# Gated attention: the compressed turn and the lump of value products move ahead of the transposition on TensorE's queue

## What is computed

```python
s_c = einsum('bqghd,bngd->bghqn', qb, kc) * scale      # 31 compressed keys
p_c = masked_softmax(s_c, cmp_end <= t)
o_c = einsum('bghqn,bngd->bqghd', p_c, vc)
...
p_s = masked_softmax(einsum(qb, k_g) * scale, valid_s)  # selected keys
o_s = einsum('bghqk,bgqkd->bqghd', p_s, v_g)
...
p_w = masked_softmax(einsum(qb, kw) * scale, valid_w)   # window keys
o_w = einsum('bghqk,bkgd->bqghd', p_w, vw)
out = gb[..., 0:1] * o_c + gb[..., 1:2] * o_s + gb[..., 2:3] * o_w
```

## Time and profile before

| | us |
|---|---|
| median of 3 runs | 2261.6 (2260.36 to 2263.69) |
| profiled execution, its own time | 2260.86 |
| its span | 2259.6 |
| TensorE busy in the span | 2201.7 (97%) |
| VectorE, ScalarE, GpSimd busy | 1341.6, 560.7, 199.8 |
| the stage of the change, from the first logits to the last lump | 853.6 to 1020.7 |

### The profile page before, as it was taken

The page is one execution under the profiler, slowest core; times in us unless marked ns, Lnnn a source line. Parts: engine busy times, 40 slices in busy tenths (PEclk is TensorE's granted clock), DMA queues, the critical chain, the costliest instruction groups (busy, mean ns, idle before and its releaser), DMA issues.

```text
span 2259.6 us, 29545 instructions
## 1 busy us (share of the span) xinstructions
PE 2201.7 (97%) x10990; PEld 1583.5 (70%) x10990; DVE 1341.6 (59%) x3432; ACT 560.7 (25%) x1421; POOL 199.8 (9%) x210
## 2 busy tenths in 40 slices
PE   9999999999999998999999999999999999999988
PEld 7776578888888885558888888888867633343333
DVE  6777766656566667876665665767776522222224
ACT  2223431101001206772110000323573111111111
POOL 0013430000000002330000000000020011111101
PEclk9999999999999999999999999999999999999999
DMA  5211032232222320002222222232205999999997
GB/s 212 75 57 47 13 124 86 83 94 86 82 94 88 121 75 20 1 1 75 83 86 94 84 85 94 77 103 64 63 13 219 356 416 423 423 422 424 423 425 325
DMA packets 60207, 346.54 MB, mean 153 GB/s; under 512 B 9248, under 2 KB 10144, under 8 KB 42208
## 3 DMA queue, kind: packets, MB, share of 16 engines
q1 hardware_dynamic: 55360, 335.03, 39.7%
q0 software_dynamic: 3840, 6.46, 0.8%
q10 hardware_dynamic: 864, 3.15, 0.3%
HBM read 337.59 MB, written 17.30 MB: 157 GB/s over the span
## 4 chain that ended last, share of the span: by engine, by line
PE 89%; DMA 6%; DVE 3%; ACT 1%; issue 1%; DVEq 0%; SPq 0%; POOLq 0%; ACTq 0%
PE bank L636 30%; PE bank L642 8%; PE bank L649 8%; PE bank L657 8%; PE bank L3097 7%; DMA places<-in_experts 5%; PE bank L3105 4%; PE bank L625 2%; PE bank L3054 2%; PE bank L1125 2%; PE bank L1137 2%; PE bank L1109 2%; PE bank L3070 1%; PE bank L499 1%; PE bank L731 1%; PE bank L1332 1%
## 5 line engine op out<-in xcount | busy, mean ns | idle before, releaser
L3097 PE MATMUL bank<-places,xT 128*64 128x512 f32 x832 | 185.1, 593 | 12.9 <-DMA places<-in_experts 12.9
L3306 DVE TENSOR_SCALAR square<-bank,mt 128x256 f32<-128x256 f32 x32 | 15.5, 484 | 284.8 <-ACT rope L3209 284.8
L3097 PEld LDWEIGHTS bank<-places,xT 128*64 128x64 f32 x832 | 60.4, 137 | 132.2 <-issue 118.9
L1992 DVE TENSOR_TENSOR third<-first,bank 128x256 f32<-128x256 f32 x106 | 44.6, 421 | 151.3 <-PE bank L636 150.5
L636 PE MATMUL bank<-u,ring 128*128 128x256 f32 x540 | 130.3, 381 | 1.1 <-DVE y_ab L2026 1.1
L636 PE MATMUL bank<-h,ring 128*128 128x256 f32 x512 | 121.0, 379 | 0.0
L636 PE MATMUL bank<-h_sums,w_sum 128*128 128x256 f32 x512 | 120.9, 379 | 0.0
L636 PEld LDWEIGHTS bank<-u,ring 128*128 128x128 f32 x540 | 101.2, 190 | 17.8 <-issue 3.3
L2685 POOL TENSOR_SCALAR exps<-exps,small,gates 128x128 f32<-128x128 f32 (+1 forms) x64 | 55.9, 874 | 652.9 <-DVE small L2479 652.9
L636 PE MATMUL bank<-u_mlp,ring 128*128 128x256 f32 x480 | 113.4, 379 | 0.0
L636 PE MATMUL bank<-u_mlp_sums,w_sum 128*128 128x256 f32 x480 | 113.4, 379 | 0.0
(11 more groups left out here) (560 smaller groups left out, 4394.0 us busy)
## 6 DMA issues: line engine op xcount, KB each, us to landing
places<-in_experts SPq DMA_DIRECT2D x56, 2048.0 KB, 35.0
ring<-in_dense SPq DMA_DIRECT2D x216, 512.0 KB, 4.2
places<-in_experts SPq DMA_DIRECT2D x40, 1024.0 KB, 23.1
x<-in_experts SPq DMA_DIRECT2D x11, 1024.0 KB, 24.8
w<-in_experts SPq DMA_DIRECT2D x10, 1024.0 KB, 29.6
consts<-in_experts SPq DMA_DIRECT2D x10, 1024.0 KB, 30.4
x<-in_experts SPq DMA_DIRECT2D x4, 2048.0 KB, 37.3
consts<-in_consts SPq DMA_DIRECT2D x1, 2310.5 KB, 16.5
```

Source lines behind the costliest of these rows:

```text
L3097: ins = k.pe.matmul(bank[a * CAP:(a + 1) * CAP, :], xT[:, kk % 4, kk // 4, :], w[:, (2 * (kk % 2) + a) * EH:(2 * (kk % 2) + a + 1) * EH], ...
```

## The change

In each step of `pe_nsa` the compressed turn (at A3) and the lump (at A0 and A3) are issued behind the unit's logits and ahead of the transposition, where before they came behind the transposition. The lists of the other engines stay as they are.

```diff
@@ pe_nsa
         if m < 8 and at == 0:
             pe_cmp_logits(k, m)
+        if m < 8 and at == 3:
+            pe_cmp_turn(k, m)
+        if step >= 4 and (step - 4) % 3 == 2:
+            pe_nsa_values(k, NSA_UNITS[step - 4][-1])
         if 0 <= step - 3 < len(NSA_UNITS):
             pe_nsa_turn(k, step - 3)
-        if m < 8 and at == 3:
-            pe_cmp_turn(k, m)
         if m < 7 and at == 4:
             pe.wait_ge(s["scaled"], SCALED["c"] + CQ + m + 2)
             pe_rope(k, k.ch7, ("cq", m + 1), k.yc[:, CQ + m + 1, :])
         if m < 8 and at == 4:
             pe_cmp_values(k, m)
-        if step >= 4 and (step - 4) % 3 == 2:
-            pe_nsa_values(k, NSA_UNITS[step - 4][-1])
```

## The result

The changed kernel takes 2274.8 us in the median of 7 runs (2270.09 to 2279.51), the kernel before 2261.6 (7 runs, 2259.3 to 2267.78): a ratio of 1.0051, interval 1.0033 to 1.0068, slower by 13.2 us. The profiled execution took 2271.68. I had forecast 2268.9, and no more than 2272. The direction and the mechanism held, the size did not: 13.2 us instead of 7.3.

What follows compares the result with a forecast made beforehand. No engine is full, TensorE is nearest; loops +5.7, opening +0.6, and end +0.5 and +0.5 sum to +7.3 us on the profiled 2260.86, or 2268.9 us for the median; range 2263.5 to 2272.

Steps and rivals of the forecast that it cites:

- the loop: Each m: TensorE to ScalarE to TensorE twice, 20.98 us against 20.16 on average before; seven loops cost +5.7 us.
- the opening: First A3, no lump: the compressed turn moves ahead and waits for VectorE's weights, delaying the first rotary product by 0.6 us.
- the end: At m = 7: +0.5 us waiting for `u`, and +0.5 from the compressed values on, 13.1 us against 12.5.
- A3 comes back at the rotary product: The 1.56 us saved at A3 return as a 1.54 us stall for `p_cmpT` before A4's rotary product: net nothing.
- A0's delay reaches the A3 lump: A0's transposition starts 2.30 us later, ScalarE with it; the A3 lump starts at 901.78, not about 900.64.
- Rival 2: Both shifts cancel, about 2262.5 us, needing ScalarE's 6.07 us to be 1.1 shorter; chance 0.15 together with a shorter loop.
- ScalarE's idle time before the A0 copies: At A0 ScalarE stands idle about 2 us, so that masks up to 2 us late cost nothing.
- the wait for `u`: At m = 7 the compressed values also wait for `u`, copied 0.49 us behind `p_cmpT`: +0.5 us.
- Rival 3: Three stalls per m could lower the clock; a tenth of the stage at half speed costs some 15 us, 2284; chance 0.03.
- The bounds: Without delays the loop is 20.7 and the sum +5.3; with ScalarE 0.1 us longer per stretch, 21.2 and +8.7.
- Rival 1: The gap is simply filled: TensorE's 13.0 us of waits at A3 and A0 are gained, 2249.2 us; chance 0.08, wholly or partly.

Runs made afterwards that it cites:

- one: Against the changed kernel, the A0 lump goes back behind its transposition, so only A3 has the new order: 2262.4 us, ratio 0.9994 to the kernel before.
- two: Against the changed kernel, compressed turn and A3 lump go back behind the transposition, only the A0 lump stays ahead: 2263.0 us, ratio 0.9997.
- five: The changed kernel run again, unaltered, for a larger sample beside the kernel before: 2273.3 us, ratio 1.0053.
- six: The changed kernel plus seven keep-warm products (matmuls nobody reads) in front of the last compressed values alone: 2271.0 us, ratio 1.004.
- eight: Only A3's lump ahead, plus ScalarE's `p_cmpT` copy moved before its A3 copies and `u` right behind them, against the kernel before: 2251.8 us, ratio 0.9954.
- seven: The changed kernel, both lumps ahead, plus ScalarE's `p_cmpT` copy before its A3 copies and `u` right behind them: 2260.5 us, ratio 0.9992 to the kernel before.

## Why the prediction was wrong in size and right in cause

The path was right: a loop from TensorE to ScalarE and back, twice per m. Of the sum, +7.3 us, these terms were mis-sized: the loop (20.98 forecast, 21.21 measured: +1.6 us over seven), the opening (-0.25), the end at full clock (+0.1), and the clock behind the last gap, which the sum put at nothing (+1.4). That gives the stage's 10.2. The 3 us that are left up to 13.2 are most likely the clock's spread from one execution to the next, for which my range had little room.

*A3 comes back at the rotary product.* Right: 1.35 us of wait there at each of the seven, 1.54 forecast, and A3 alone changes nothing (one).

*A0's delay reaches the A3 lump.* Right: block 3's transposition waits 0.61 us, the lump 0.32, in sum 0.93 where I had 1.1. Rival 2 (both shifts cancel) holds only if one half is left out (one, two).

*The loop of 20.98 us.* The term that missed by most. It is 21.21: rotary product to A0 lump 5.89 instead of 5.72 (it takes 0.93 us instead of 0.86 after a wait, and the lump follows the compressed logits 1.03 behind instead of 0.94), from a transposition to the copies twice 0.64 instead of 0.59; ScalarE's stretches and the delays came out within 0.03. The two terms that were short were read from places where TensorE's work ran through without a wait. Seven times 0.23 is 1.6 us. ScalarE's idle time before the A0 copies, which I had put at about 2 us, is 2.68.

*The opening and the end.* The opening cost 0.35 instead of 0.6. At the end the wait for `u` is there, 0.5 us as forecast (1.84 against 1.35), and the rest is +0.6 at full clock, where I had 0.5.

*Rival 3, the clock.* I wrote that the new stalls are no longer than 1.4 us. That was wrong by my own sum: a stall of 1.54 plus 0.5 for `u` at m = 7 is 2.0, and the trace shows 1.84. Behind it the clock fell, +1.4 us (five, six). The size that I gave the rival, 15 us, was ten times too large; it took place once and not in every m.

*The bounds.* For the other 3 us of the first difference no step of the kernel is known. The median of seven runs moves with the clock that each execution was granted: within the runs of each of the two kernels the time goes up by some 2 us for each 0.001 that the mean clock is lower, and the lowered clock lies in other places from one execution to the next. A straight line through each kernel's runs meets clock 1.00 at 2259.2 for the kernel before (52 runs in the first two groups) and at 2268 for the changed one (13 runs): 8.7 us at equal clock. In the second sample the medians are 10.3 apart. Both fit a cost of about 9 us at equal clock and 10 with the fall at the stage's end; that the rest is chance is the likeliest reading, and not shown. My range took in the bounds of the sum and little for this, though the kernel before shows it too once more runs are there (2259.25 to 2275.48). None of the changed kernel's 13 runs reached a mean clock of 1.000, where 8 of those 52 did; that fits a fall at the stage's end each time, and isn't proven by it.

*Rival 1, the gap is filled.* Its condition, slack on ScalarE, was the right one for A3: given that slack by two moves in ScalarE's list, and with the A0 lump left where it was (eight), the gap is filled, 2251.8 against the 2249.2 that I had put beside the rival. For the change as it stands, with both lumps ahead, the same two moves don't bring it about (seven, 2260.5).

## What to carry to other kernels

Work moved into a gap delays everything that stood in front of it: follow the moved-back group's consumers round to where they meet the same engine again, and write the loop's length as a sum of rows, since two edits that cost nothing alone can add up once neither leaves the other its slack. Where a lump covers no wait, leave it behind the transposition, so that it covers the copies instead. And before moving work on the bounding engine, look at the copies that another engine makes at the end of its step though the data are there at its start: moved alone they brought nothing, but only with them out of the way did the new order at A3 bring its 11 us.

## What the hardware showed

TensorE, busy 97% of the span, has its clock lowered for some us now and then: mean clocks of 1.000 to 0.993 for one and the same kernel, with some 2 us for each 0.001. Whether it falls differs from one execution to the next, but the places come again. In the eleven profiles it fell at 292 to 298 us in three, at 280 to 292 in two, at 808 to 822 in five, at 1790 to 1814 in three and at 214 to 218 in one, all outside the stage of the change, and in the last few us of the program in all eleven.

A gap of 1.8 us at the stage's end was followed by the lower clock in each of the three profiles that had it, the gaps of 1.35 us in front of the rotary products in none. The length of the last gap doesn't decide alone: in seven's profile the clock fell behind a gap of 1.27 us at the stage's opening, where ten other profiles with the same gap stay at full clock:

```profile
859.78 3.21 PE L1109 MATMUL bank<-y_c 64*128 64x512 f32 x12 [1.27 <-DVE small L2298]
```

The same twelve instructions take 1.88 us in the kernel before.

From the end of ScalarE's copy to TensorE's waiting instruction it is 0.14 to 0.15 us in the places read here, at L731 (911.49 to 911.64) and at L1137 (905.31 to 905.46).
